# Second MLP product of a gated trunk layer: eight half-size block products become seven, in a Strassen scheme

## The reference

```python
hn = rms_norm(h, norm_mlp[l])          # (512, 1024)
a = jax.nn.relu(hn @ w_mlp_in[l])      # (512, 4096)
h = h + (a * a) @ w_mlp_out[l]         # (512, 1024)
return rms_norm(h, norm_final)
```

## Time and profile before

| what | value |
|---|---|
| median of the runs | 990.69 us (990.22 to 991.94) |
| the profiled execution: its own time | 992.16 us |
| its span, first to last instruction | 990.4 us |
| TensorE busy | 959.5 us, 97% of the span |
| VectorE busy | 478.8 us, 48% |
| ScalarE busy | 349.9 us, 35% |
| moved by DMA | 92.60 MB, 93 GB/s on average |

### The profile page before, as it was taken

One profiled execution on the slowest core, in us unless ns is written; L12 is line 12 of the kernel. 1 busy time (PEld: TensorE's weight loads), 2 busy tenths in 40 slices (PEclk: granted clock), 3 DMA queues, 4 the chain that ended last, 5 costly groups with the idle time before them and its releaser, 6 DMA issues.

```text
span 990.4 us, 11650 instructions
## 1 busy us (share of the span) xinstructions
PE 959.5 (97%) x4677; PEld 779.0 (79%) x4677; DVE 478.8 (48%) x873; ACT 349.9 (35%) x562; POOL 14.0 (1%) x38
## 2 busy tenths in 40 slices
PE   7999999999999999999999999999999999999996
PEld 5778777777776788889877668888888888888885
DVE  5632666433457654678134436643344434334536
ACT  4431555434424224336244422442144123213411
POOL 4000000000000000000000000000000000000000
PEclk8999999999999999999999999999999999999999
DMA  8311221122102162334422222222222332222212
GB/s 279 94 55 65 86 85 43 44 85 85 58 29 86 46 252 85 107 128 132 144 85 85 86 85 85 85 85 85 85 86 95 127 118 86 85 85 85 88 41 85
DMA packets 44206, 92.60 MB, mean 93 GB/s; under 512 B 1677, under 2 KB 1769, under 8 KB 44153
## 3 DMA queue, kind: packets, MB, share of 16 engines
q1 hardware_dynamic: 42584, 86.54, 26.1%
q0 software_dynamic: 1568, 5.32, 1.6%
HBM read 89.76 MB, written 2.10 MB: 93 GB/s over the span
## 4 chain that ended last, share of the span: by engine, by line
PE 87%; DVE 7%; ACT 3%; issue 1%; DMA 1%; SPq 0%; ACTq 0%; DVEq 0%
PE bank L1066 76%; DVE w_lo L796 2%; PE bank L1239 1%; DVE conv_acc L816 1%; PE bank L1079 1%; PE bank L1190 1%; PE bank L1177 1%; PE bank L1133 1%; PE bank L1217 1%; ACT w_hi L587 1%; PE bank L1160 1%; DMA stage<-in_w_in 1%; PE bank L1204 1%; PE bank L1145 1%; PE bank L1178 1%
## 5 line engine op out<-in xcount | busy, mean ns | idle before, releaser
L1066 PE MATMUL bank<-act_hi,w_hi 128*128 128x512 f32 (+2 forms) x624 | 247.5, 397 | 2.4 <-DVE act_lo L892 2.4
L1066 PE MATMUL bank<-act_hi,w_lo 128*128 128x512 f32 (+2 forms) x624 | 242.2, 388 | 0.0
L1066 PE MATMUL bank<-act_lo,w_hi 128*128 128x512 f32 (+2 forms) x624 | 242.0, 388 | 0.0
L796 DVE TENSOR_TENSOR w_lo<-stage,w_hi 128x1024 fp32r<-128x1024 f32 x156 | 184.0, 1221 | 113.1 <-ACT w_hi L587 113.0
L587 ACT ACTIVATE w_hi<-stage 128x1024 fp32r<-128x1024 f32 x156 | 156.5, 1051 | 186.2 <-PE bank L1066 180.3
L1066 PE MATMUL bank<-w_hi,act_hi 128*128 128x512 f32 x448 | 177.2, 395 | 4.1 <-DVE act_lo L892 3.3
L1066 PE MATMUL bank<-w_hi,act_lo 128*128 128x512 f32 x448 | 175.5, 392 | 0.0
L1066 PE MATMUL bank<-w_lo,act_hi 128*128 128x512 f32 x448 | 175.3, 391 | 0.0
L1066 PEld LDWEIGHTS bank<-act_hi,w_hi 128*128 128x128 f32 x624 | 118.7, 190 | 24.9 <-issue 2.6
L1066 PEld LDWEIGHTS bank<-act_hi,w_lo 128*128 128x128 f32 x624 | 118.4, 190 | 24.0
L1066 PEld LDWEIGHTS bank<-act_lo,w_hi 128*128 128x128 f32 x624 | 118.7, 190 | 22.1
(11 more groups left out here) (221 smaller groups left out, 916.0 us busy)
## 6 DMA issues: line engine op xcount, KB each, us to landing
stage<-in_w_in SPq DMA_DIRECT2D x22, 1024.0 KB, 5.0
stage<-in_w_mlp_in SPq DMA_DIRECT2D x16, 1024.0 KB, 5.3
stage<-in_w_mlp_out SPq DMA_DIRECT2D x16, 1024.0 KB, 5.1
stage<-in_w_xkv SPq DMA_DIRECT2D x8, 1024.0 KB, 5.0
stage<-in_w_mix_out SPq DMA_DIRECT2D x4, 1024.0 KB, 5.1
stage<-in_w_xq SPq DMA_DIRECT2D x4, 1024.0 KB, 5.2
stage<-in_w_xo SPq DMA_DIRECT2D x4, 1024.0 KB, 5.1
x_tok<-in_x SPq DMA_DIRECT2D x4, 512.0 KB, 10.9
```

The costliest lines, as they stand in the source:

```text
L796: dve.tensor_tensor(w_lo[:, r:r + 2, :], src, w_hi[:, r:r + 2, :].bitcast(F32), ALU.subtract)\
L1066: ins = pe.matmul(dst, still[q], moving[q], start=(k == 0 and q == 0), stop=(k == nk - 1 and q == 2))
```

## The change

The second MLP product of a round is (512 x 1024) times (1024 x 1024). It is cut into 2 x 2 blocks: tokens in halves of 256, inner columns into even and odd tiles, output columns into halves of 512. Before, the eight block products are done as they stand. Now seven products are done, q0 to q6, each of 4 slabs, on sums of blocks (the variant of Strassen's scheme by Winograd):

- **Weights.** Four of the seven right-hand operands (q1, q2, q4, q6) are differences of blocks, made by VectorE in place in `stage` (`weight_sum`), before they are split. `stage` has three buffers in the MLP. The number of slabs to split in a round's second product goes from 16 to 28. As many lots are loaded as before.
- **Activations.** For every pair of tiles VectorE makes four sums of 128x256 (`act_sums`), ScalarE three further high parts, VectorE three further low parts.
- **Products.** A product is two halves (m = 0, 1) of 12 matmuls, each into a bank of its own, among banks 2 to 7 in turn.
- **Folds.** VectorE adds each half into a sum in SBUF (`fold`): `p1`, `p5`, `p6`, `p7`, or a quarter of `h_tok`. The four `p` sums run over all rounds; in round 3 eight additions of 128 x 1024 (`add_to`, each waiting for the one before) bring them into `h_tok`.
- **The end.** Rows of tokens 0 to 255 are complete after q5, the others after q6; the norms are hung there.
- Tiles get other places in SBUF, `relu` and `relu2` are replaced by `ff`, in which relu, square and sums are done in place.

The unit of the second product has 14 pairs now.

```diff
-STAGES = 2
+STAGES = 3
+PRODUCTS = 7
+PRODUCT = ((0, 0), (1, 0), (2, 0), (4, 2), (3, 1), (5, 3), (6, 0))
+SUMMED = {1: (1, 0), 2: (2, 0), 4: (2, 1), 6: (3, 0)}
...
-            (f"mlp_out{2 * r}", "w_mlp_out", r * DM, KT, 0, NT),
-            (f"mlp_out{2 * r + 1}", "w_mlp_out", r * DM, KT, HALF_W, NT),
+            (f"mlp_out{r}", "w_mlp_out", r * DM, 4 * PRODUCTS, 0, 2),
...
-        after(group_end(n, i) - 1, ("norm", 3 * NT + 2 + i))
+        after(HALF_AT[(n, i % 2, 5 if i < 2 else 6)], ("norm", 3 * NT + 2 + i))
+    for v in range(FF // P // 2):
+        n, j = UNIT[f"mlp_in{v // 2}"], 2 * (v % 2) + 1
+        after(group_end(n, j) - 1 + (1 if v % 4 < 3 else 0), ("act_sums", v))
...
         steps += b + [("half", i)]
+        if in_products(n):
+            steps.append(("fold", i))
+            steps += a + [("split_weights", p) for p in pairs.get(i, [])]
+            continue
...
+    for p in split:
+        if p % 2 == 0 and p in SUM_NO:
+            i = steps.index(("split_weights", p - 1)) + 1
+            steps[i:i] = [("weight_sum", p), ("weight_sum", p + 1)]
...
+                elif step == "act_sums":
+                    u = n % 4
+                    act.wait_ge(s_asum, 3 * n + 1)
+                    copy(act2_hi[:, 2 * u, TOK // 2:TOK], ff[:, 2 * u + 1, TOK // 2:TOK]).then_inc(s_sh, 1)
+                    act.wait_ge(s_asum, 3 * n + 2)
+                    copy(sa_hi[:, u, :], ff[:, 2 * u, :]).then_inc(s_sh, 1)
+                    act.wait_ge(s_asum, 3 * n + 3)
+                    copy(sb_hi[:, u, :], ff[:, 2 * u + 1, 0:TOK // 2]).then_inc(s_sh, 1)
...
+            def weight_sum(pair):
...
+                dve.tensor_tensor(dst, stage[LOTS[plus][3]][:, rows, :], stage[LOTS[minus][3]][:, rows, :],
+                                  ALU.subtract).then_inc(s_wsum, 1)
...
+            def add_to(dst, more):
+                link(dve.tensor_tensor(dst, dst, more, ALU.add))
+
+            def fold(i):
...
+                dst = (p1, p5, p6, quarter(0, 1), p7, quarter(0, 0), quarter(1, 0))[q][:, m, :]
+                src = two[1 + (PRODUCTS * r + q) % 3][:, m, :]
...
+                dve.wait_ge(s_half, i + 1)
+                if r == 0 and q in (0, 1, 2, 4):
+                    dve.tensor_copy(dst, src).then_inc(s_fold, 1)
+                else:
+                    dve.tensor_tensor(dst, src, dst, ALU.add).then_inc(s_fold, 1)
+                if last and m == 1:
+                    dve.wait_ge(s_fold, folds(r, q, m))
+                    if q == 0:
+                        add_to(quarter(0, 0), p1[:])
+                    elif q == 1:
+                        add_to(quarter(1, 1), p5[:])
+                        add_to(quarter(0, 1), p5[:])
+                    elif q == 2:
+                        add_to(p6[:], p1[:])
+                        add_to(quarter(0, 1), p6[:])
+                    elif q == 4:
+                        add_to(p7[:], p6[:])
+                        add_to(quarter(1, 1), p7[:])
+                        add_to(quarter(1, 0), p7[:])
...
+                dve.tensor_tensor(a22, a21, a22, ALU.add).then_inc(s_asum, 1)
+                dve.tensor_tensor(a21, a11, a21, ALU.subtract)
+                dve.wait_ge(s_asum, 3 * v + 1)
+                dve.tensor_tensor(a11, a22, a11, ALU.subtract).then_inc(s_asum, 1)
+                dve.wait_ge(s_asum, 3 * v + 2)
+                dve.tensor_tensor(a12, a12, a11, ALU.subtract).then_inc(s_asum, 1)
...
+                if PRODUCTS * r + q >= 3:
+                    pe.wait_ge(s_fold, folds(r, q, m) - 6)
+                for u in range(4):
...
+                        if u % 2 == 0:
+                            pe.wait_ge(s_low, slab // 2 + 1)
```

More of the change, by code:

```diff
@@ L43 @@
 KB = 1024
-ALIGN = 128
+ALIGN = 512
 def make_units():
@@ L88 @@
 SLAB0 = [sum(u[3] for u in UNITS[:n]) for n in range(len(UNITS) + 1)]
-GROUP0 = [sum(u[5] for u in UNITS[:n]) for n in range(len(UNITS) + 1)]
+GROUP0 = [sum(u[5] for u in UNITS[:n] if u[3] <= KT) for n in range(len(UNITS) + 1)]
 def make_halves():
@@ L99, in make_halves @@
         cs, groups = range(u[3] // 4), range(u[5])
+        if u[3] > KT:
+            halves += [(n, m, q, 0, HALF_W) for q in cs for m in groups]
+            continue
         if u[0] == "mlp_in0":
@@ L480, in _ @@
             sp.dma_start(row_a[:], norm_mix.partition_broadcast(P)).then_inc(s_row_x, 16)
[L481 to L498, removed]
-                            row += v.shape[0]
@@ new lines, in _ @@
+            held = {}
+            for lot, (n, c, half, buf) in enumerate(LOTS):
+                _, w, row0, nk, col0, _ = UNITS[n]
+                if half is None:
+                    src = weights[w][row0 + LOT * P * c:row0 + LOT * P * (c + 1), col0:col0 + HALF_W]\
+                        .rearrange("(k p) n -> p k n", p=P)
+                else:
+                    src = weights[w][row0:row0 + DM, HALF_W * half:HALF_W * (half + 1)]\
+                        .rearrange("(u two p) n -> two p u n", two=2, p=P)[c]
+                if buf in held:
+                    what, count = FREED[held[buf]]
+                    sp.wait_ge(s_low if what == "low" else s_wsum, count)
+                held[buf] = lot
+                sp.dma_start(stage[buf][:], src).then_inc(s_lot[buf], 16)
+                if lot == 0:
+                    load_x(1)
+                if lot == 1:
+                    load_x(2)
+                    load_x(3)
+                    row = 0
+                    for v in (conv_w.rearrange("j (c p) -> (j c) p", p=P), conv_b.rearrange("(c p) -> c p", p=P),
+                              b_gate.rearrange("(c p) -> c p", p=P), mlstm_norm.rearrange("(c p) -> c p", p=P)):
+                        sp.dma_start(param_rows[row:row + v.shape[0], :], v).then_inc(s_param, 16)
+                        row += v.shape[0]
@@ L1067, in half, with product @@
                                         stop=(k == nk - 1 and q == 2))
+                ins.then_inc(s_half, 1)
+            def product(i):
+                n, m, q, *_ = HALVES[i]
+                r, what = order(n), PRODUCT[q][0]
+                dst = two[1 + (PRODUCTS * r + q) % 3][:, m, :]
+                low, high = (slice(h + P * m, h + P * m + P) for h in (0, TOK // 2))
+                if PRODUCTS * r + q >= 3:
+                    pe.wait_ge(s_fold, folds(r, q, m) - 6)
+                for u in range(4):
+                    v = 4 * r + u
+                    slab = SLAB0[n] + 4 * q + u
+                    if m == 0:
+                        if u % 2 == 0:
+                            pe.wait_ge(s_low, slab // 2 + 1)
+                        if what in (0, 5, 6):
+                            pe.wait_ge(s_al, 2 * v + (1 if what == 0 else 2))
+                        else:
+                            pe.wait_ge(s_sl, 3 * v + (0, 1, 2, 2, 3)[what])
+                    hi, lo = ((act2_hi[:, 2 * u, low], act2_lo[:, 2 * u, low]),
+                              (act2_hi[:, 2 * u, high], ff_lo[:, 2 * u + 1, high]),
+                              (sa_hi[:, u, low], ff_lo[:, 2 * u, low]),
+                              (sa_hi[:, u, high], ff_lo[:, 2 * u, high]),
+                              (sb_hi[:, u, low], ff_lo[:, 2 * u + 1, low]),
+                              (act2_hi[:, 2 * u + 1, low], act2_lo[:, 2 * u + 1, low]),
+                              (act2_hi[:, 2 * u + 1, high], act2_lo[:, 2 * u + 1, high]))[what]
+                    for g, (s, w) in enumerate(((hi, w_hi), (hi, w_lo), (lo, w_hi))):
+                        ins = pe.matmul(dst, s, w[:, slab % RING, :], start=(u == 0 and g == 0),
+                                        stop=(u == 3 and g == 2))
                 ins.then_inc(s_half, 1)
@@ L1249, in _ @@
                 if step == "half":
-                    half(n)
+                    product(n) if in_products(HALVES[n][0]) else half(n)
                 elif step == "norm_turn":
```

180 lines of the change are left out of this document (133 added, 47 removed).

## The result

The changed kernel takes 996.18 us, the median of 5 runs (994.85 to 996.75), against 990.53 (990.14 to 991.94) for the kernel before in the same session. The measured ratio is 1.0049, 95% interval 1.0035 to 1.0063, that is 3.5 to 6.2 us slower; the two medians alone are 5.65 apart. The profiled execution took 996.18 us with a span of 994.5; before it was 992.16 and 990.4, so profile against profile it is +4.0, with the forecast at +3.9.

A forecast was written before the change was run, and what follows sets the result against it. TensorE alone bounds the MLP before, VectorE's queue round 3's end after; rounds 0 to 3 sum to -5.44 - 1.9 - 5.44 + 16.7 = +3.9 us, on 990.7 giving 994.6. Range 992.0 to 999.5.

The forecast's parts named there:

- matmuls removed: Second products: 24 fewer matmuls a round, 96 in all, at 0.2267 us each; 5.44 us a round, 21.8 in all.
- rounds 0 and 2: Splits stand ahead of t7 and finish before q0 begins, so nothing is lost; 5.44 us saved in each round.
- waits at q4, q5, q6 of round 3: Round 3, second product: TensorE waits 2.1, 0.7 and 0.3 us for low parts of weights from VectorE.
- What bounds it now: MLP before the change: TensorE alone for 344.79 us, matmul starts 0.2267 us apart, group boundaries free; 5.31 us behind it.
- Handover: Start of q1 in rounds 1 and 3: due at 5.3 us after t7, starts at 7.1, 1.8 lost.
- inner stall: Second first-product unit of rounds 1 and 3: the second lot's split stands behind t3's high part; 1.7 us lost.
- The additions: Round 3: eight additions of 128 x 1024 on VectorE, each waiting for the one before; 1.25 us each, 10 in all.
- The four norms in a row: End of round 3 on VectorE: each norm holds up the next fold; 3 x 5.22 + 5.29 = 20.9 us, end at 63.8.
- cheaper sums: Rival: differences and additions in SBUF cost 0.82 us in place of 1.22, round 3's queue 5.6 shorter; 989.0 us, chance 0.08.
- the full gain: Rival: no stall and norms spread as before, so all 21.8 us are gained; 968.9 us, chance 0.03.
- The clock at the new waits: Rival: TensorE's new waits in rounds 1 and 3 each bring the clock down; 999 to 1000 us, chance 0.12.
- Full durations: Rival: VectorE instructions do not overlap, 1.25 us a low part, 0.72 a fold; some 4 us more, 998.6, chance 0.15.

The follow-up runs named there:

- e1: The changed kernel with pairs counted as second lot by their number within their unit in the MLP; 987.50 us, ratio to before 0.9963.
- e4: The changed kernel with the eight additions of round 3 left out, so part of the computation is missing; 986.34 us, ratio to before 0.9951.
- e2: The changed kernel with p7's three additions behind q5's second fold and only the first norm ahead of q6's folds; 992.15 us, ratio to before 0.9999.
- e3: The changed kernel with the edits of e1 and e2 together; 983.77 us, ratio to before 0.9915.
- e5: e3 with the eight additions of round 3 moved from VectorE to GpSimd; 986.12 us, ratio to before 0.9961.
- e6: e3 with the wait for a store moved from ScalarE's square to VectorE's scaling, a norm's last step; 981.72 us, ratio to before 0.9918.
- e7: e3 with 18 matmuls of 128 columns into an unused bank ahead of the MLP's first half; 983.76 us, ratio to before 0.9937.
- e9: The kernel before the change with 18 matmuls of 128 columns into an unused bank ahead of the MLP's first half; 991.64 us, ratio 1.0010.

## Why the prediction was right

Times from t7's end are counted from 927.4, the end of the last unit before the second product (908.06 + 19.35). Waits are distances of starts less 0.2267, which is up to 0.2 more than the idle time that a row names.

| step | predicted | measured |
|---|---|---|
| matmuls removed | 0.2267 each, 5.44 a round | 38.08 for 168; e1: in all rounds |
| rounds 0 and 2 | no stall | none |
| second first-product unit, rounds 1 and 3 | 1.7 | 1.73, 1.73 |
| q1, rounds 1 and 3 | 1.8 | 1.88, 1.88 |
| waits at q4, q5, q6 of round 3 | 2.1, 0.7, 0.3 | 1.95, 0.56, 0.30 |
| fold of q5's first half begins | 42.9 after t7 | 42.96 |
| distance of the norms | 5.22 | 5.20 to 5.27 |
| end of the last norm | 63.8 after t7 | 63.99 |
| MLP | +3.9 | +4.5 |

- **What bounds it now, removed matmuls, rounds 0 and 2**: right as written. No group boundary over six banks costs anything; the earlier trace rows holds for halves of 12.
- **Handover and inner stall**: right in place, size and cause. e1 shows the cause: with the pairs counted within their unit all of them go.
- **The additions**: price 1.22 to 1.23, starts 1.26 apart against 1.25. What they cost together the prediction did not say; the expectation of e4, from the same queue, put 8.0, and e4 shows 8.5 of the 10.
- **The four norms in a row**: right, and e2 shows that 4.4 us of it are the order.
- **What was mis-sized**: the sum, by 0.6. From 714.96 to 800.41 round 1 took 85.45 in place of 81.60, 3.85 lost where I had 3.5; round 3 lost 1.88 ahead of t7 where I had 1.7; the tail is 0.2 longer. The row at 741.01 shows most of it: after a wait the first matmul lasts 0.50 (0.47 at 767.51) and its successor comes 0.33 later, not 0.2267, so each wait costs 0.1 more than its length.
- **What was luck**: that the profiled executions differ by +4.0 against a forecast of +3.9. The MLP is 4.54 longer, and the stretch ahead of it, which the sum leaves out, was 0.41 shorter in the profile after (636.75 against 637.16). The step from the profiled execution to the median did not hold: the forecast took 1.5 off, while the profiled execution of the changed kernel took 996.18, just its median. So 996.1 was met for the profiled execution, and 994.6 for the median is 1.6 low, within the range.
- **A slip in the chances**: "cheaper sums" came to 989.0, 1.7 below 990.7, which by the prediction's own bound of 2.0 is no change. Of the named cases only the full gain, 0.03, lies under "faster", which was given 0.08.
- **The clock at the new waits**: refuted. By windows of the kernel after (us; PE busy, PEld busy, DVE, ACT, POOL; granted clock; DMA share, GB/s), the waits of 1.73 and 1.88 and those of round 3:

```profile
736.00:741.00 5.00, 3.44 (x16) 2.51 (x14) 2.66 (x4) 3.48 (x5) 0.00 (x0) 1.00 0.00 0
760.00:768.00 8.00, 6.28 (x28) 4.95 (x27) 6.07 (x11) 4.48 (x7) 0.00 (x0) 1.00 0.00 0
936.00:960.00 24.00, 21.80 (x95) 17.47 (x94) 23.72 (x24) 8.16 (x8) 0.00 (x0) 1.00 0.13 44
```

  The clock is 1.00, that is 2.4 GHz, in each. What the Trainium skill ("TensorE: Matmul & The Clock Gate", section on the second failure mode) tells of another kernel, in bf16, that cycling through banks brings the clock down, is not seen here in pieces of 38.08 us over six banks.
- **Full durations**: refuted; a pair of low parts lasts 2.35 and what follows it starts 2.27 after it, as in the earlier trace rows. Only instructions that wait for the one just before give up the overlap (967.84, 2.48 for two).
- **Cheaper sums in SBUF**: refuted, 1.22 a difference and an addition.
- **The full gain of 21.8** is not had even with both edits: e3 has 8.1 of it. 2.4 are TensorE's waits in round 3's second product (1.49, 0.56, 0.33); the rest, about 11, lies behind TensorE's last matmul (16.3 us in e3, 5.31 before), in three additions and four norms where one norm stood.

## What to carry to other kernels

A scheme that takes matmuls away pays with block sums on another engine; before counting the gain, write out that engine's queue to the last instruction, since its end and not TensorE's may be the kernel's. Look for rules in a schedule that read an absolute number (here `p % 4`): a unit of another length shifts everything behind it, and correcting that was worth 8.2 us, more than the change had cost. Take what the longest tail waits for first: two edits of a few lines turned 1.0049 of the time before into 0.9915.

## What the runs showed of the hardware that was not expected

- **VectorE and GpSimd exclude each other on SBUF operands** (e5): 4.19 us for two low parts instead of 2.35, 2.40 for an instruction of 0.22, while folds from PSUM keep their length.
- **The same wait sometimes lowers the clock and sometimes not.** TensorE waits 2.4 us before the MLP in the changed kernel and in e3 alike, behind the eight transposes of the norm. Windows of the kernel after, then of e3:

```profile
628.00:630.00 2.00, 2.00 (x11) 2.00 (x11) 1.70 (x10) 2.00 (x4) 0.00 (x0) 0.80 0.97 347
630.00:632.00 2.00, 2.00 (x8) 2.00 (x7) 1.93 (x4) 0.14 (x1) 0.00 (x0) 0.50 0.37 142
```

```profile
628.00:630.00 2.00, 2.00 (x12) 2.00 (x13) 1.72 (x9) 2.00 (x4) 0.00 (x0) 1.00 0.96 329
630.00:632.00 2.00, 2.00 (x14) 2.00 (x13) 1.91 (x4) 0.23 (x1) 0.00 (x0) 1.00 0.46 177
```

  The first 36 matmuls took 8.05 to 8.07 us in the profiles of before, after, e2, e5 and e6 and 6.48 to 6.51 in those of e1, e3 and e4: 1.6 us that belong to no edit. The waits of 1.73 to 1.95 us of the changed kernel, e2 and e4, and one of 2.00 in e5, lowered it in none of their windows.
- **Part of what sets executions apart lies far ahead of the MLP.** The edits of e1 to e7 all lie in the MLP or at its start, yet 36 full-width matmuls at 90 us took 8.28 us in the profiles of e3, e4 and e7, 9.90 or 9.91 in after, e1, e2 and e6, and 11.06 in e5; in the kernel before 9.59, in e9 10.97. The clock tells them apart. One window of e7, then of e9:

```profile
92.00:94.00 2.00, 2.00 (x11) 1.65 (x10) 0.00 (x0) 0.00 (x0) 0.00 (x0) 1.00 0.00 0
```

```profile
92.00:94.00 2.00, 2.00 (x7) 1.52 (x6) 0.00 (x0) 0.00 (x0) 0.00 (x0) 0.50 0.00 0
```

  Here TensorE did not wait before the fall: from 86.7 to 90 it worked on matmuls of 12 columns, in e7 as in e9, and in e9 the granted clock was 0.82 from 88 to 90 and 0.50 from 90 to 96. The next 24 matmuls began at 98.97 in e7, 100.46 in e3 and 102.18 in e5. Other falls are seen at 304 us (before) and at 181 and 308 us (e5), whose MLP begins 5.2 us later than that of e3. These are one profile a kernel: how often each fall comes is not known, nor why it comes in some executions only.
- **The matmul after a wait is slow by itself**: 0.47 to 0.50 instead of 0.39 us at a clock of 1.00, the next start about 0.1 us late, at all seven waits of the changed kernel.
